# The combine of a top-4-of-32 expert layer: a float32 matmul per piece, or three fp32r products of its split operands

## The reference, cut to what matters

```python
logits = (t @ w_router + b_router).astype(jnp.float32)
top_v, top_e = lax.top_k(logits, TOP_K)
gates = jax.nn.softmax(top_v, axis=-1)
...
def expert_block(args):
    xb, e = args
    hh = xb @ w1[e] + b1[e]
    glu, lin = jnp.split(hh, 2, axis=-1)
    glu = jnp.minimum(glu, SWIGLU_LIMIT)
    lin = jnp.clip(lin, -SWIGLU_LIMIT, SWIGLU_LIMIT)
    act = glu * jax.nn.sigmoid(SWIGLU_ALPHA * glu) * (lin + 1.0)
    return act @ w2[e] + b2[e]
...
y = jax.ops.segment_sum(out * row_gate[:, None].astype(out.dtype), row_tok, num_segments=T + 1)[:T]
```

## Time and profile before

| what | us |
|---|---|
| median of 3 runs | 1418.36 |
| lowest and highest run | 1416.41, 1418.98 |
| span of the profiled execution, first to last instruction | 1417.7 |
| of it ahead of the first gather of the experts | 376 |
| expert loop and last combine | 376 to 1405 |
| last norm and stores | 1405 to 1418 |

### The profile page before, as it was taken

The page is one execution under the profiler, slowest core; times in us unless marked ns, Lnnn a source line. Parts: engine busy times, 40 slices in busy tenths (PEclk is TensorE's granted clock), DMA queues, the critical chain, the costliest instruction groups (busy, mean ns, idle before and its releaser), DMA issues.

```text
span 1417.7 us, 18156 instructions
## 1 busy us (share of the span) xinstructions
PE 1293.6 (91%) x6994; PEld 632.8 (45%) x6994; DVE 508.9 (36%) x907; ACT 202.4 (14%) x354; POOL 138.0 (10%) x100
## 2 busy tenths in 40 slices
PE   5999997869499999999999999999999999999995
PEld 4788897748232433333333333333333333333341
DVE  3455888546623132222223132222222232222313
ACT  2332011010310111101011111111110111111012
POOL 6102266611300000000000000000000000000000
PEclk9999998979699999999999999999999999999998
DMA  9632386684689999999999999999999999999940
GB/s 316 199 121 76 119 268 209 226 329 176 243 350 413 386 398 398 393 402 385 415 385 416 382 398 398 383 414 384 413 388 411 387 405 389 386 406 392 417 169 35
DMA packets 123892, 467.05 MB, mean 329 GB/s; under 512 B 7440, under 2 KB 54064, under 8 KB 90864
## 3 DMA queue, kind: packets, MB, share of 16 engines
q1 hardware_dynamic: 116848, 455.37, 81.6%
q0 software_dynamic: 1616, 6.65, 1.5%
q10 hardware_dynamic: 5392, 4.54, 1.0%
HBM read 460.84 MB, written 5.70 MB: 329 GB/s over the span
## 4 chain that ended last, share of the span: by engine, by line
PE 84%; DVE 10%; ACT 2%; issue 2%; DMA 2%; DVEq 0%; SPq 0%; ACTq 0%
PE bank L1601 31%; PE bank L1631 16%; PE bank L1577 11%; PE bank L1256 8%; PE bank L1557 5%; PE bank L1420 4%; PE bank L1408 2%; PE bank L1619 1%; DVE rest L978 1%; ACT rest L719 1%; DVE split L931 1%; DMA ring<-w_in 1%; PE bank L1595 1%; DVE rest L1174 1%; DVE rest L1002 1%
## 5 line engine op out<-in xcount | busy, mean ns | idle before, releaser
L1601 PE MATMUL bank<-ring,rest 128*64 128x512 f32 x2048 | 452.0, 594 | 0.0
L1174 DVE TENSOR_TENSOR rest<-rest,bank 128x512 f32<-128x512 f32 (+1 forms) x198 | 133.8, 682 | 498.4 <-PE bank L1577 498.3
L1601 PEld LDWEIGHTS bank<-ring,rest 128*64 128x64 f32 x2048 | 144.3, 137 | 286.9 <-issue 281.2
L1631 PE MATMUL bank<-ring,rest 128*64 128x512 f32 x1024 | 226.8, 595 | 11.1 <-ACT rest L719 11.1
L1577 PE MATMUL bank<-rest 128*128 128x512 f32 (+1 forms) x396 | 196.2, 617 | 24.8 <-DVE rest L1174 23.7
L1256 PE MATMUL bank<-rest,ring 128*128 128x288 f32 (+1 forms) x512 | 125.2, 405 | 16.2 <-DMA ring<-w_in 16.2
L1631 PEld LDWEIGHTS bank<-ring,rest 128*64 128x64 f32 x1024 | 70.7, 137 | 146.6 <-issue 127.9
L1577 PEld LDWEIGHTS bank<-rest 128*128 128x128 f32 (+1 forms) x396 | 51.3, 161 | 166.4 <-DVE rest L1174 97.5
L1256 PEld LDWEIGHTS bank<-rest,ring 128*128 128x128 f32 x512 | 98.0, 193 | 40.9 <-DMA ring<-w_in 16.2
L715 ACT ACTIVATE rest<-rest 128x512 f32<-128x512 f32 x32 | 20.1, 630 | 575.1 <-DVE rest L1192 575.1
L1420 PE MATMUL bank<-split 128*128 128x288 f32 x576 | 86.8, 314 | 10.2 <-DVE split L980 5.7
(11 more groups left out here) (296 smaller groups left out, 779.2 us busy)
## 6 DMA issues: line engine op xcount, KB each, us to landing
ring<-w SPq DMA_DIRECT2D x384, 1024.0 KB, 8.4
ring<-w_in SPq DMA_DIRECT2D x12, 1024.0 KB, 13.4
ring<-k_t SPq DMA_DIRECT2D x8, 1024.0 KB, 5.4
ring<-v_c SPq DMA_DIRECT2D x8, 1024.0 KB, 12.8
ring<-w_xk SPq DMA_DIRECT2D x4, 1024.0 KB, 5.1
ring<-w_xv SPq DMA_DIRECT2D x4, 1024.0 KB, 5.1
ring<-w_out SPq DMA_DIRECT2D x4, 1024.0 KB, 5.9
ring<-w_xq SPq DMA_DIRECT2D x4, 1024.0 KB, 5.8
```

Source lines behind the costliest of these rows:

```text
L1174: v.tensor_tensor(dst, dst, ps[6 + q % 2][0:R, :], ALU.add).then_inc(comb_free, 1)
L1601: last = t.matmul(out, slots[:, k, :], w[:, col], start=False, stop=(k == KT - 1))
L1631: last = t.matmul(ps[2 + ds][CAP * cg:CAP * cg + CAP, :], actT[:, a * P + CAP * cg:a * P + CAP * cg + CAP], w[:, cg, 512 * ds:512 * ds + 5 ...
```

## The change

Both operands of the combine are held in two parts. `selGT` and `outp` become pairs of fp32r tiles: part 0 is the value rounded to fp32r, which ScalarE's copies now write, and part 1 is the remainder, which VectorE subtracts from the bank (`split_output`, at the end of each expert's turn). Each piece of the combine becomes three products: remainder of the gates times upper output, upper gates times remainder, upper times upper. TensorE waits for one semaphore, `outp_split`, three counts per expert, in place of `outp_done` and `selgt_done`; its wait for `b2` goes. `b2` is loaded into a tile of its own, later, behind the three parts of the tokens (`h_split`), and VectorE splits it ahead of the loop. Clears of both tiles are doubled. Some tiles move, and the count `prod_done` is folded into `lin_done`.

```diff
@@ -213,17 +213,19 @@
         glu, lin, sig, act = (m(7680 + 512 * i, 512) for i in range(4))
         htmp = [m(7680, D), m(8704, D), cells(xT_at + D, xT_at + 2 * D)]
         junk = m(0, 6 * 512, 2, TT, 512)
-        pick_t = m(10752, TT * TOPK * NE, TT, TOPK, NE)
+        pick_t = m(10240, TT * TOPK * NE, TT, TOPK, NE)
         actT = m(9728, 512)
-        selGT = m(10240, 384)
-        selG = m(10752, 384, TT, P)
-        sel = m(11136, 192).bitcast(BF16).rearrange("p (t s) -> p t s", t=TT)
-        oh = [m(11328 + 32 * i, 32).bitcast(BF16) for i in range(2)]
+        selG = m(10240, 384, TT, P)
+        selGT = [places_r[M0 + 10752][:, 384 * i:384 * i + 384] for i in range(2)]
+        h_at = xT_at + KT * T
+        sel = cells(h_at + 2 * D, h_at + 2 * D + 192).bitcast(BF16).rearrange("p (t s) -> p t s", t=TT)
+        oh = [cells(h_at + 2 * D + 192 + 32 * i, h_at + 2 * D + 224 + 32 * i).bitcast(BF16) for i in range(2)]
         b1s = m(11520, 1024).bitcast(BF16)
         frow = m(12544, D)
         xg = [xT_at + i * 1024 for i in range(2)]
         xg = [cells(a, a + 1024).rearrange("p (k s) -> p k s", k=KT) for a in xg]
-        outp = cells(xT_at + KT * T, xT_at + KT * T + 1024)
+        outp = [places_r[h_at][:, D * i:D * i + D] for i in range(2)]
+        b2_f = m(7680, D)
 
 
         ring_in = [sem(f"ring_in{s}") for s in range(SLOTS)]
@@ -269,8 +271,8 @@
 
         oh_done, sel_done, selg_done, selgt_ps, selgt_done, xg_ps, xg_done = map(
             sem, "oh_done sel_done selg_done selgt_ps selgt_done xg_ps xg_done".split())
-        glu_done, lin_done, sig_done, prod_done, act_done, actt_ps, actt_done, outp_done, comb_ps, comb_free = map(
-            sem, "glu_done lin_done sig_done prod_done act_done actt_ps actt_done outp_done comb_ps comb_free".split())
+        glu_done, lin_done, sig_done, act_done, actt_ps, actt_done, outp_done, outp_split, comb_ps, comb_free = map(
+            sem, "glu_done lin_done sig_done act_done actt_ps actt_done outp_done outp_split comb_ps comb_free".split())
         hx_zero, selgt_zero, rounds_done, fin_sum, fin_std, y_ready, round_step = map(
             sem, "hx_zero selgt_zero rounds_done fin_sum fin_std y_ready round_step".split())
 
@@ -537,10 +539,8 @@
                 pool.wait_ge(h_hi, tt + 1)
                 pool.tensor_tensor(htmp[tt][0:R], htmp[tt][0:R], hx[0:R, 0, tt, :], ALU.subtract).then_inc(h_rest, 1)
 
-            pool.wait_ge(outp_done, 2)
-            pool.dma_start(outp[0:NE], b2).then_inc(b2_in, 16)
-
-            pool.wait_ge(h_tok, TT)
+            pool.wait_ge(h_split, TT)
+            pool.dma_start(b2_f[0:NE], b2).then_inc(b2_in, 16)
             pool.dma_start(frow, fin_g.partition_broadcast(P)).then_inc(grow_in, 16)
 
 
@@ -706,7 +706,7 @@
 
             act_e.wait_ge(gt_ps, 1)
             act_e.wait_ge(selgt_zero, 1)
-            a.copy(selGT[0:NE], ps[7][0:NE, 0:384]).then_inc(selgt_done, 1)
+            a.copy(selGT[0][0:NE], ps[7][0:NE, 0:384]).then_inc(selgt_done, 1)
 
             def turn(g):
                 for j in range(BODY):
@@ -718,11 +718,11 @@
                     act_e.wait_ge(actt_ps, n + 1)
                     a.copy(actT, ps[4][:, :]).then_inc(actt_done, 1)
                     act_e.wait_ge(selgt_ps, n + 2)
-                    a.copy(selGT, ps[5][:, 0:384]).then_inc(selgt_done, 1)
+                    a.copy(selGT[0], ps[5][:, 0:384]).then_inc(selgt_done, 1)
 
                     act_e.wait_ge(units_used, (n + 1) * EXP_UNITS)
-                    a.copy(outp[:, 0:512], ps[2][:, :]).then_inc(outp_done, 1)
-                    a.copy(outp[:, 512:1024], ps[3][:, :]).then_inc(outp_done, 1)
+                    a.copy(outp[0][:, 0:512], ps[2][:, :]).then_inc(outp_done, 1)
+                    a.copy(outp[0][:, 512:1024], ps[3][:, :]).then_inc(outp_done, 1)
 
             with act_e.Fori(0, TURNS) as i:
                 turn(i)
@@ -1057,7 +1057,8 @@
                 else:
                     v.tensor_copy(b1s[64:96], b1f[64:96]).then_inc(b1_split, 1)
                     dve.wait_ge(b1_split, 1)
-                    v.memset(selGT, 0.0).then_inc(selgt_zero, 1)
+                    v.memset(selGT[0].bitcast(F32), 0.0)
+                    v.memset(selGT[1].bitcast(F32), 0.0).then_inc(selgt_zero, 1)
 
             def x_rows(half):
 
@@ -1080,7 +1081,8 @@
             x_rows(1)
             dve.wait_ge(y_sq, 2 * TT)
             v.tensor_tensor(ysum, ysq[:, 0, :], ysq[:, 1, :], ALU.add).then_inc(y_sum, 1)
-            v.memset(outp, 0.0).then_inc(outp_done, 2)
+            v.memset(outp[0].bitcast(F32), 0.0)
+            v.memset(outp[1].bitcast(F32), 0.0).then_inc(outp_done, 2)
             dve.wait_ge(y_std, 1)
             link(v.reciprocal(yrs, yrs))
             dve.wait_ge(lt_ps, 1)
@@ -1161,6 +1163,22 @@
 
             v.memset(selG, 0.0).then_inc(selgt_ps, 1)
             v.memset(most, 0.0).then_inc(comb_free, 2)
+
+            dve.wait_ge(selgt_done, 1)
+            v.tensor_tensor(selGT[1][0:NE], ps[7][0:NE, 0:384], selGT[0][0:NE], ALU.subtract).then_inc(outp_split, 1)
+            dve.wait_ge(b2_in, 16)
+            dve.wait_ge(outp_done, 2)
+            link(v.tensor_copy(outp[0][0:NE], b2_f[0:NE]))
+            v.tensor_tensor(outp[1][0:NE], b2_f[0:NE], outp[0][0:NE], ALU.subtract).then_inc(outp_split, 2)
+
+            def split_output(n, r):
+
+                dve.wait_ge(selgt_done, n + r + 2)
+                v.tensor_tensor(selGT[1], ps[5][:, 0:384], selGT[0], ALU.subtract).then_inc(outp_split, 1)
+                for half in range(2):
+                    q = slice(512 * half, 512 * half + 512)
+                    dve.wait_ge(outp_done, 2 * n + 3 + half)
+                    v.tensor_tensor(outp[1][:, q], ps[2 + half][:, :], outp[0][:, q], ALU.subtract).then_inc(outp_split, 1)
 
             def add_combined(c, pieces=range(2 * TT)):
 
@@ -1192,13 +1210,14 @@
                     v.tensor_scalar(glu, ps[0][:, :], LIMIT, None, ALU.min).then_inc(glu_done, 1)
                     v.tensor_scalar(lin, ps[1][:, :], LIMIT, -LIMIT, ALU.min, ALU.max).then_inc(lin_done, 1)
                     dve.wait_ge(glu_done, n + 1)
-                    dve.wait_ge(lin_done, n + 1)
-                    v.scalar_tensor_tensor(lin, lin, 1.0, glu, ALU.add, ALU.mult).then_inc(prod_done, 1)
-                    dve.wait_ge(prod_done, n + 1)
+                    dve.wait_ge(lin_done, 2 * n + 1)
+                    v.scalar_tensor_tensor(lin, lin, 1.0, glu, ALU.add, ALU.mult).then_inc(lin_done, 1)
+                    dve.wait_ge(lin_done, 2 * n + 2)
                     dve.wait_ge(sig_done, n + 1)
                     v.tensor_tensor(act, lin, sig, ALU.mult).then_inc(act_done, 1)
                     if j % 2:
                         add_combined(n + r, range(3, 2 * TT))
+                    split_output(n, r)
 
             def last_combine(g, r):
 
@@ -1217,7 +1236,8 @@
             def one_round(r):
                 dve.wait_ge(selgt_ps, r * NE + 1)
                 dve.wait_ge(round_step, r)
-                v.memset(selGT, 0.0).then_inc(selgt_done, 1)
+                v.memset(selGT[0].bitcast(F32), 0.0).then_inc(selgt_done, 1)
+                v.memset(selGT[1].bitcast(F32), 0.0).then_inc(outp_split, 3)
                 with dve.Fori(0, TURNS) as i:
                     turn(i, r * TURNS + i, r)
                 last_combine((r + 1) * TURNS, r)
@@ -1574,8 +1594,10 @@
                 for q in pieces:
                     tt, half = q // 2, q % 2
                     pe.wait_ge(comb_free, 2 * TT * c + q + 1)
-                    t.matmul(ps[6 + half][0:ROWS[tt], :], selGT[:, tt * P:tt * P + ROWS[tt]],
-                             outp[:, half * 512:(half + 1) * 512], start=True, stop=True).then_inc(comb_ps, 1)
+                    for n, (g_part, o_part) in enumerate(((1, 0), (0, 1), (0, 0))):
+                        last = t.matmul(ps[6 + half][0:ROWS[tt], :], selGT[g_part][:, tt * P:tt * P + ROWS[tt]],
+                                        outp[o_part][:, half * 512:(half + 1) * 512], start=(n == 0), stop=(n == 2))
+                    last.then_inc(comb_ps, 1)
 
             def turn(g, r):
                 for j in range(BODY):
@@ -1602,8 +1624,7 @@
                         last.then_inc(units_used, 1)
                         if k == 3:
 
-                            pe.wait_ge(outp_done, 2 * (n + 1))
-                            pe.wait_ge(selgt_done, n + r + 1)
+                            pe.wait_ge(outp_split, 3 * (n + r + 1))
                             combine(n + r, range(2 * TT) if j % 2 == 0 else range(3))
 
                     if j % 2:
@@ -1634,12 +1655,10 @@
                         last.then_inc(units_used, 1)
 
             def last_combine(g, r):
-                pe.wait_ge(outp_done, 2 * (g * BODY + 1))
-                pe.wait_ge(selgt_done, g * BODY + r + 1)
+                pe.wait_ge(outp_split, 3 * (g * BODY + r + 1))
                 combine(g * BODY + r)
 
```

(1 more changed line is left out.)

## The result

The changed kernel takes 1400.84 us, the median of four runs (1399.74 to 1403.93), against 1417.38 for the four runs of the kernel before that go with them (1415.63 to 1418.98). The ratio is 0.9884, with a 95% interval of 0.9864 to 0.9904, so the change saves 16.5 us (14 to 19). The forecast was 7.7. The profiled execution took 1399.74; its span is 1398.0, against 1417.7.

What follows compares the result with a forecast made beforehand. PE (TensorE) was taken to set the time. Start 0.9 plus end 0.2 minus combine saving 17.9 gave -16.8 us; clock falls of 9.1 made it -7.7, from 1418.4 to 1410.7 us, range 1400 to 1420.

Steps and rivals of the forecast that it cites:

- the number of falls: Clock falls behind the standstill ahead of the odd experts' sixth piece: seven of 16, 1.3 us each, 9.1 us lost.
- rival 1: Expert loop: the clock stays at 1.00, giving 1401.6 us (1396 to 1403); chance 0.25.
- the saving per pair: Combine in the expert loop: seven pieces on the path per pair, 0.16 us saved each; 17.9 us over 16 pairs.
- DVE's activation chain, which does not move: Odd expert's second half: the addition PE awaits keeps its time, so the standstill grows from 1.48 to 1.8 us.
- rival 3: Expert loop: the weight stream becomes the bound, 62.9 us a pair, 1411 us in all; chance 0.05.
- PE waits for no split inside the loop: New VectorE subtractions, three per expert, end about 5 us before PE wants them; cost nothing.
- `b2` is covered: Ahead of the first combine: the later load and split of b2 cost 0, with 3 us of cover.
- The start: Ahead of the first gather: the output tile's clear comes twice, costing 0.9 us.
- the end: Behind the last expert: PE also waits for a half's subtraction, less four shorter pieces; net cost 0.2 us.
- Rival 4: Combine: products not fp32r in effect, or weight loads not overlapped, adding 190 us; chance 0.05 with everything unforeseen.
- Rival 2: Expert loop: the clock falls in nearly every odd expert, 20.8 us lost against 16.8 saved, 1422.4 us; chance 0.20.

Runs made afterwards that it cites:

- before_stall: The kernel before (float32 combine) with one more VectorE instruction ahead of the odd experts' last three additions; 1424.87 us, ratio 1.0061.
- sixth_float32: The changed kernel with the odd experts' sixth piece as one float32 matmul of the upper parts, remainders left out there; 1405.72 us, ratio 0.9911.
- two_products: The changed kernel without the product of the gates' remainder and the upper output in each piece; 1394.67 us, ratio 0.9843.
- fill_stall: The changed kernel with three unread products run in the odd experts' standstill between fifth and sixth piece; 1396.1 us, ratio 0.9863.
- pairs_clear: The changed kernel, odd pieces dealt four and two, output clears moved under the first gather, W1's middle pieces issued two at a time; 1385.57 us, ratio 0.9769.

## Why the prediction was wrong

The sign and nearly all mechanisms held; the size did not. -7.7 was forecast, -16.5 measured, and two terms of the sum erred to the same side.

**The failed step is the number of falls.** The step "The new standstill lies between 1.48, which was always harmless, and 1.82, which was not, and nearer to the latter", and from it "seven of 16, 9.1 us". The standstill was right (1.8 predicted, 1.86 measured), and so was the price (1.3, measured 1.27). But the harmful 1.82 was one event, read as a threshold: the same standstill is harmless in five of the twelve traces, and in this loop 1.82 was harmless 16 times, with float32 pieces (before_stall). Four falls came, 5.1 us: 4.0 of the error. The text had rival 1 note that the row was from a different stage, and then let it count in full. That falls came in some of the 16 and not in others is as forecast; no row gave the seven, which was a guess. Its other argument, that fp32r "streams less time per piece", is not borne out: with a float32 sixth piece the falls are three in place of four, and with float32 pieces alone they come as well, at 2.08.

**The second is the saving per pair**, "Seven by 16 pairs by 0.16 is 17.9 us". It was 22.1. The piece was nearly right (0.17 saved, a product of 0.227 where 0.23 was taken). What the step missed stands behind the odd expert's W1, where 0.39 was saved in place of 0.16. First, the last piece is followed by the transposes, whose weight load waited for the float32 matmul and now runs beside the last product: 0.16 a pair, 2.6 us, which sixth_float32 gives back. Second, "DVE's activation chain, which does not move", did move: it is 0.07 shorter where the count was folded, 1.1 us. The rest of the 4.2 us is the 0.01 per piece of the even combine.

The Trainium skill, "TensorE: Matmul & The Clock Gate", section "Back-to-back issue gap", would have had 0.216 for a product; the measured 0.227 lies nearer to the rows of the split projections.

**Right, point by point.** PE still sets the time, with no idle time of L1623; rival 3 fell, and in two_products the stream fed a still shorter loop. The pieces are three fp32r records; the even combine was put near 5.0 (4.98) and the first odd half near 2.65 (2.64). PE waits for no split inside the loop. `b2` is covered. The start costs 1.06 (0.9 predicted), the end 0.17 (0.2). Rival 4 fell with the 0.227. Rival 2, a fall in nearly every odd expert, did not happen here, but it is what two_products does.

**Rival 1** gave 1401.6, close to the 1400.84, by another way: it has the clock at 1.00 throughout, and the trace shows four falls under a larger saving. Without falls, and with the filler, the kernel takes 1396.1 (fill_stall). That its time came so close is luck: it has the saving 4.2 too small and the falls, 5.1, at nothing, and the two all but cancel.

What stays open is why the falls after the change come in every fourth pair. The standstills of the pairs with and without a fall look alike in the traces (1.84 to 1.86), as those of the earlier trace rows do; no run here tells them apart.

## What to carry to other kernels

Before a shorter product is counted as pure gain, ask what PE waits for next: where the wait hangs on another engine, each tenth cut ahead of it lengthens the standstill, and a standstill has a price of its own in clock (here 1.27 us a fall). Take the price and the length at which it is due from the same stage and from more than one event, for a single fall is no threshold. Or test it with a filler: products that nobody reads took the falls out of this kernel. Better than a filler is to deal the work out so that the standstill ends earlier: four pieces ahead and two behind, in place of three and three, gave 0.7 us a pair before the change and 0.5 after it.

## What the runs showed of the hardware that was not expected

- Standstills of PE between 1.82 and 2.32 us, with matmuls on both sides, took this loop from no fall of the clock to one per standstill, with falls in float32 and in fp32r kernels. Near 1.85 the same standstill came with a fall and without one. The Trainium skill, "TensorE: Matmul & The Clock Gate", section "A second HAM failure mode: psum-queue depth-cycling", tells of a kernel that lost its clock by small pauses between groups of matmuls; the trace agrees for the longer of these pauses and not for the shorter ones.
- The weight load of a float32 transpose ran beside the fp32r product ahead of it (0.23 before its first matmul), and did not beside a float32 matmul, where it stood idle 0.84 (before, sixth_float32).
- A change between the matmuls of W1, which use the array by column halves, and the combine's full-width products costs 0.3 to 0.4 us there and back (pairs_clear). That the column halves are the cause is not shown; no run separates them from the change of banks and operands.
